# Layer-2 mixers: attention output with features on partitions, scores divided before they are transposed

## The chip, the cores and the metric

The kernel runs on one NeuronCore of a Trainium2 chip. The metric is the device time of one launch in microseconds, the median of several runs. TensorE does the matrix products and the 128 x 128 transposes (into PSUM), VectorE and ScalarE the elementwise work, GpSimd some copies and small products between SBUF buffers, and SyncE issues the DMAs.

## The reference, cut to what matters

Two layers follow each other over 1024 tokens of width 1024. The second layer normalizes its input, projects it, runs three mixers side by side (a windowed attention with a sink, a state-space mixer "ssd" and a gated delta-rule mixer "gdn"), joins their outputs, multiplies them by one output matrix, and adds the normalized result to its input; a feed-forward block follows.

```
s = einsum('bcikgd,bcjkd->bckgij', qc, kb) * (ATT_HEAD_DIM ** -0.5)
s = s - slopes * dist                       # alibi; invalid keys -inf
p = softmax(concatenate([s, sink], -1))[..., :band]
att = einsum('bckgij,bcjkd->bcikgd', p, vb) # 4 heads of 64, 2 kv heads
...
mix = concatenate([att, ssd, gdn], axis=-1) @ w_out      # 256 + 512 + 256 columns
x = x + rmsnorm(mix, post_mix_norm)
```

The change touches the making of `att` and how `att`, `ssd` and `gdn` become the stationary side of the product with `w_out`.

## The kernel before, in words

The whole program is one launch of several stages. The stage in question is `layer2_mixers` (L2185 and on). It works on tiles of 128 tokens, eight of them, in ten steps: `tiles(tile)` calls `tile(n, i, t)` on each engine with n, i = n-1 and t = n-2. The **front** of tile n (attention, the ssd mixer, the preparation of gdn), the **chain** of tile i (the gdn triangular solve by doubling, block size 2, 4, 8, 16, 32, 64, and its state) and the **output product** of tile t (48 float32r matmuls of 128 x 512, as high and low parts) are interleaved. Every engine runs a written order; semaphores with names (`Steps`: `tensF.wait(v, "att", n)` waits until TensorE has done `att` of tile n) tie them. Step 0 has only a front, step 1 a front and a chain, step 8 only a chain and an output; after it stands `end()`.

The chain has two products per level: `level_t(b)` makes T_b, ScalarE copies it, `level_x(b)` makes X_b, VectorE subtracts it (`V`) and turns it (`W`). In the text T64 and X64 are the products of level 64, VT64 is VectorE's copy of X64 (L2778), W the product of `KBG` and `VT` that follows (`wt`), VN the next (`vn`).

TensorE's gaps are filled with output matmuls: `fill(at)` issues those that the table `FILL` gives for that place (`FILL_FIRST` in step 2, `FILL_END` in step 8; in step 1 up to two warming matmuls each). Half 0 of a tile's product begins in one step at "x16" and ends at "end"; its second half starts inside "end", at matmul 24, once ScalarE has copied half 0 out of PSUM (`pc0`, L2454), and this copy waits until VectorE has added the previous tile's residual (`x2`, L2738).

Attention of tile n, in order: four products of queries and keys into PSUM banks 1 and 2 (`scores`), VectorE scales them and adds the bias (`swab`, L2844), maximum (L2847) and differences; ScalarE exponentials with row sums (`e0` to `e3`, L2600) and the sink's (`es`, L2618); TensorE transposes the undivided scores (L3255, `ptr`, right after the level-32 products), ScalarE copies them to `PTR` (`pt`, L2633), TensorE multiplies `PTR` (stationary, 128 columns) by the values (moving, 64 columns), two heads ahead of the ssd product with the state (`yo`, the off-diagonal product) and two heads behind W. VectorE computes the denominator and its reciprocal (L2914, L2916) and writes `att = product * 1/den` with tokens on partitions into `M` (L2927).

`M` holds the 1024 mixer outputs of one tile: 256 of attention, 512 of ssd, 256 of gdn. In the next step TensorE transposes the first six chunks of 128 (`mtrm`) and the last two (`mtrg`, L3179), ScalarE copies them as float32r (`mtm` L2575, `mtg` L2570) and VectorE makes the low part (`mlo` L2835, `mglo` L2722). On VectorE, L (the exponential of the decays `DEC`, made by ScalarE at L2624, `decayed()`) is needed by `nc0` to `nc3` (L2882); in step 0 ScalarE calls `decayed()` behind `pt`, in later steps ahead of it.

## Time and profile before

| | us |
|---|---|
| runs | 2250.68, 2253.72, 2257.84 |
| median of 3 | 2253.72 |
| profiled execution, its time | 2252.55 |
| its span in the profile | 2250.8 |
| TensorE busy over the span | 2207.3 (98%) |
| VectorE busy | 1580.2 (70%) |
| ScalarE busy | 916.0 (41%) |
| GpSimd busy | 260.7 (12%) |
| granted TensorE clock, mean | 0.993 |

Times in the trace are microseconds from the start of the span. Matmul rows overlap, since each shows a matmul until its result is out; the cost of one in a run of them is the distance between starts. An fp32 matmul leaves two rows (records), a transpose and a float32r matmul one. The mixer stage starts at 1286.7 (first transpose of step 0) and the steps' first chain products (T2) stand at 1308.21, 1345.28, 1381.55, 1416.73, 1451.91, 1487.09, 1522.27 and 1557.45; the steady steps 3 to 7 last 35.18 us each.

### The profile page before, as it was taken

To read this page: it belongs to the slowest core of one execution; us is meant where nothing else is said; L and a number is where in the kernel's file an instruction comes from. 1 tells how busy PE (TensorE), PEld (TensorE's weight loads), DVE (VectorE), ACT (ScalarE), POOL (GpSimd) and SP (SyncE) were. 2 spreads that over 40 slices of the span, in tenths; PEclk is the share of its full clock that TensorE was granted. 3 is DMA by queue.
4 is the path that set the end of the run, shared out by engine and by line. 5 is a ranking of instruction groups with operands and counts; after the bars stand their busy time and mean duration, and the time that the engine had idled before them with its cause. 6 is when DMAs were issued, how large, how long until landed. Compare 5 with 4: busy or idle time off the path is not lost. (4 is left out here: it accounts for less than half of the span.)

```text
span 2250.8 us, 34288 instructions
## 1 busy us (share of the span) xinstructions
PE 2207.3 (98%) x13052; PEld 1816.6 (81%) x13052; DVE 1580.2 (70%) x2212; ACT 916.0 (41%) x1672; POOL 260.7 (12%) x266
## 2 busy tenths in 40 slices
PE   8999999999999999999999989999999999999997
PEld 7888888888888888887887767887888888888886
DVE  5657668876665545657687798888798777765557
ACT  5443444343333331233344455555533333324444
POOL 0222232100000000001232232322020000000000
PEclk9999999999999999999999999999999999999999
DMA  4111111134333264433232442323235444448655
GB/s 153 47 38 57 38 50 45 66 132 158 122 113 112 93 248 182 159 113 116 92 113 84 152 169 72 123 77 114 97 129 192 163 158 163 158 157 301 215 181 184
DMA packets 106952, 289.06 MB, mean 128 GB/s; under 512 B 9692, under 2 KB 35388, under 8 KB 102332
## 3 DMA queue, kind: packets, MB, share of 16 engines
q1 hardware_dynamic: 106812, 287.14, 36.4%
q8 instruction: 94, 1.54, 0.3%
q14 instruction: 46, 0.38, 0.0%
HBM read 205.01 MB, written 82.10 MB: 128 GB/s over the span
## 5 line engine op out<-in xcount | busy, mean ns | idle before, releaser
L124 PE MATMUL psG<-h_hi,w_hi 128*128 128x512 f32 (+1 forms) x624 | 164.4, 395 | 4.3 <-DVE features_T L1879 3.9
L124 PE MATMUL psG<-h_hi,w_lo 128*128 128x512 f32 (+1 forms) x624 | 162.2, 392 | 0.0
L124 PE MATMUL psG<-h_lo,w_hi 128*128 128x512 f32 (+1 forms) x624 | 162.2, 393 | 0.0
L455 POOL TENSOR_TENSOR sb_w<-sb_left 128x128 f32<-128x128 f32 (+3 forms) x96 | 96.9, 1014 | 320.8 <-DVE sb_left L582 320.8
L124 PEld LDWEIGHTS psG<-h_hi,w_hi 128*128 128x128 f32 x624 | 110.1, 188 | 25.8 <-DVE features_T L1879 4.7
L124 PEld LDWEIGHTS psG<-h_hi,w_lo 128*128 128x128 f32 x624 | 112.0, 189 | 20.4 <-DVE w_lo L155 0.2
L124 PEld LDWEIGHTS psG<-h_lo,w_hi 128*128 128x128 f32 x624 | 111.6, 189 | 20.2 <-issue 0.5
L582 DVE TENSOR_TENSOR_SCAN sb_left<-sb_left 128x128 f32<-128x128 f32 (+3 forms) x96 | 102.6, 1076 | 2.1 <-ACT sb_left L468 1.4
L155 DVE TENSOR_TENSOR w_lo<-w_raw,w_hi 128x1024 fp32r<-128x1024 f32 x48 | 58.6, 1223 | 55.0 <-ACT w_hi L150 55.0
L150 ACT CAST w_hi<-w_raw 128x1024 fp32r<-128x1024 f32 x48 | 50.3, 1050 | 114.9 <-PE psG L124 62.1
L2028 POOL TENSOR_TENSOR features_T<-m_bias_both 128x512 f32<-128x512 f32 x10 | 16.3, 1635 | 677.3 <-DMA m_bias_both<-in_proj_pairs 630.7
L590 DVE TENSOR_TENSOR sb_w_lo<-psT,sb_w_hi 128x512 fp32r<-128x512 f32 (+1 forms) x80 | 50.0, 625 | 62.1 <-ACT sb_w_hi L476 61.7
L468 ACT ACTIVATE sb_left<-psA 128x128 f32<-128x128 f32 (+3 forms) x96 | 47.2, 491 | 101.0 <-PE psA L124 52.7
L476 ACT CAST sb_w_hi<-psT 128x512 fp32r<-128x512 f32 (+1 forms) x80 | 43.5, 544 | 87.1 <-PE psT L721 87.0
L1051 ACT ACTIVATE features_T<-features_T 128x512 f32<-128x512 f32 x54 | 34.2, 633 | 88.3 <-DVE features_T L1132 87.8
L1916 DVE SCALAR_TENSOR_TENSOR features_T<-features_T,p_par 128x1024 f32<-128x1024 f32 x42 | 55.6, 1323 | 11.5 <-ACT features_T L1780 10.4
L3746 DVE TENSOR_TENSOR h_ffn_lo<-ff_raw_up,h_ffn_hi 128x512 fp32r<-128x512 f32 x49 | 33.7, 690 | 40.8 <-ACT h_ffn_hi L3612 20.6
L3746 DVE TENSOR_TENSOR w_lo<-ff_raw_up,w_hi 128x512 fp32r<-128x512 f32 x39 | 27.0, 692 | 47.0 <-ACT w_hi L3704 47.0
L3746 DVE TENSOR_TENSOR features_T<-ff_y,features_T 128x512 f32<-128x512 f32 x50 | 34.4, 689 | 35.7 <-PE ff_y L124 35.7
L124 PE MATMUL m_ps<-m_w_hi,m_a_hi 128*128 128x512 f32 x128 | 54.1, 433 | 0.4 <-ACT m_raw L2454 0.4
L3612 ACT CAST ff_a_hi<-features_T 128x512 fp32r<-128x512 f32 x40 | 24.6, 625 | 69.6 <-PE psH L124 29.5
L1132 DVE TENSOR_TENSOR features_T<-mg_y,features_T 128x512 f32<-128x512 f32 x45 | 31.0, 689 | 30.4 <-PE mg_y L124 29.9
(657 smaller groups left out, 5931.9 us busy)
## 6 DMA issues: line engine op xcount, KB each, us to landing
w_raw<-in_units SPq DMA_DIRECT2D x76, 512.0 KB, 4.2
w_raw<-hidden_blocks SPq DMA_DIRECT2D x77, 256.0 KB, 2.8
merge_gates<-features_T SPq DMA_DIRECT2D x12, 1024.0 KB, 7.4
merge_gates<-merge_gates SPq DMA_DIRECT2D x12, 1024.0 KB, 4.8
features<-features_T SPq DMA_DIRECT2D x24, 512.0 KB, 6.2
w_spare<-in_units SPq DMA_DIRECT2D x22, 512.0 KB, 4.4
down_sums<-w_spare SPq DMA_DIRECT2D x22, 512.0 KB, 3.3
hidden_blocks<-features_T SPq DMA_DIRECT2D x11, 1024.0 KB, 3.9
```

The source lines that it names most:

```text
L124: return pe.matmul(out, lhs, rhs, start=first, stop=last, skip_group_check=True)
L150: act.copy(self.hi[c % 2][:] if dest is None else dest, self.raw[c % 2][:]).then_inc(self.hi_done, 1)
L155: dve.tensor_tensor(self.lo[c % 2][:] if dest is None else dest, self.raw[c % 2][:], hi.bitcast(F32), ALU.subtract).then_inc(self.lo_done, 1)
L455: pool.tensor_tensor(w, left_chunk(S, 1), left_chunk(S), ALU.subtract).then_inc(w_ready, 1)
L468: act.activation(left_chunk(S), A[:, 0:row_chunk(S)[1]], ACT.Sigmoid, scale=-1.0).then_inc(keep_done, 1)
L476: act.copy(w_hi[n % 2][:, 0:m], wT[n % 2][:, 0:m]).then_inc(w_hi_done, 1)
L582: dve.tensor_tensor_scan(back, back, back, start, ALU.mult, ALU.min).then_inc(scan_done, 1)
L590: dve.tensor_tensor(w_lo[n % 2][:, 0:m], wT[n % 2][:, 0:m], w_hi[n % 2][:, 0:m].bitcast(F32), ALU.subtract).then_inc(w_lo_done, 1)
L1051: act.activation(dst, src, func).then_inc(gated, 1)
L1132: TT = lambda o, a, b, op: dve.tensor_tensor(o, a, b, op)
L1916: dve.scalar_tensor_tensor(acc[r], raw[r][:, t:t + T], par[:, c, t:t + 1], acc[r], ALU.mult, ALU.add).then_inc(step if t else conv_out, 1)
L3746: TT = lambda o, a, b, op: dve.tensor_tensor(o, a, b, op)
```

## The change

1. Attention is made with features on partitions. The values (64 columns) are the stationary side and `PTR` (128 columns) the moving one; head 0 and head 3 go to bank 1 (partitions 0 to 63 and 64 to 127), heads 2 and 1 to bank 2. The rows of `w_out` for attention are put into this order on the host. All four heads are computed in one place, behind the fill "wt" and ahead of W; the off-diagonal product `yo` moves behind W.
2. The scores are divided by the denominator before they are transposed: VectorE's `den` and `rden` move from behind `sd1` and `xdec` to a place ahead of `nc0`, and `pn` (1024 columns) is added there. The score transposes now wait for `pn` and stand behind T64.
3. The two attention chunks need no transpose: ScalarE copies them from banks 1 and 2 to `A0_HI` (`ah`, float32r) and VectorE subtracts (`att`) to `A0_LO`, three buffers each. `M` shrinks to 768 columns, `mtrm`, `mtm` and `mlo` to four chunks.
4. The fill "x64" is emptied into "t64", which now stands ahead of T64 with seven output matmuls.

```diff
+                if front:
+                    tensF.wait(a, "att", n)
+                    if n >= 3:
+                        tensA.wait(a, "a6", n - 3)
+                    scalF.done("ah", a.copy(A0_HI[n % 3][:], PS[:, 1:3, 0:P]))
...
-                    scalG.done("mtm", a.copy(A6_HI[i % 2][:], bank(3, 2)[:, 0:6 * P].rearrange("p (c t) -> p c t", c=6)))
+                    scalG.done("mtm", a.copy(A4_HI[i % 2][:], bank(3).rearrange("p (c t) -> p c t", c=4)))
...
                 if front:
+                    scalF.wait(v, "es", n)
+                    vectF.done("den", tt(den[:], sums[:], es[:], ALU.add))
+                    vectF.wait(v, "den", n)
+                    vectF.done("rden", v.reciprocal(rden[:], den[:]))
+                    vectF.wait(v, "rden", n)
+                    vectF.done("pn", tt(SS[:], SS[:], per(rden[:], AH, 256), ALU.mult))
                     scalL.wait(v, "L", n)
...
-                    scalF.wait(v, "es", n)
-                    vectF.done("den", tt(den[:], sums[:], es[:], ALU.add))
-                    vectF.wait(v, "den", n)
-                    vectF.done("rden", v.reciprocal(rden[:], den[:]))
...
-                    tensF.wait(v, "att", n)
-                    tensG.wait_last(v, "mtrm", n)
-                    vectF.wait(v, "rden", n)
-                    vectF.done("att", tt(heads(M[:, 0:256], AH), heads(PS[:, 1, 0:256], AH), per(rden[:], AH, 64), ALU.mult))
+                    scalF.wait(v, "ah", n)
+                    vectF.done("att", tt(A0_LO[n % 3][:], PS[:, 1:3, 0:P], A0_HI[n % 3][:].bitcast(F32), ALU.subtract))
...
-                def attention(first):
-                    for h in (first, first + 1):
-                        kv = 64 * (h // 2)
-                        mm(PS[:, 1, 64 * h:64 * h + 64], PTR[:, 2 * h], VP[:, kv:kv + 64], True, False)
-                        x = mm(PS[:, 1, 64 * h:64 * h + 64], PTR[:, 2 * h + 1], GA[:, 256 + kv:320 + kv], False, True)
+                def attention():
+                    for pair in ((0, 1), (2, 3)):
+                        for m in range(2):
+                            for h in pair:
+                                kv = 64 * (h // 2)
+                                values = GA[:, 256 + kv:320 + kv] if m else VP[:, kv:kv + 64]
+                                x = mm(PS[half(h), 2 if h in (1, 2) else 1, 0:P], values, PTR[:, 2 * h + m], m == 0, m == 1)
                     return x
...
-                    turn(tensG, "mtrm", 3, [M[:, c * P:(c + 1) * P] for c in range(6)])
+                    turn(tensG, "mtrm", 3, [M[:, c * P:(c + 1) * P] for c in range(4)])
...
-                if front:
-                    for h in range(AH):
-                        if h % 2 == 0:
-                            scalF.wait(pe, f"e{h + 1}", n)
-                        for m in range(2):
-                            x = pe.transpose(PS[:, 1 + h // 2, (2 * (h % 2) + m) * P:(2 * (h % 2) + m + 1) * P], SS[:, h, m * P:(m + 1) * P], C["ident"][:])
-                    tensF.done("ptr", x)
                 if chain and not front:
                     turn_h(1)
                 fill("t64")
                 level_t(64)
+                if front:
+                    vectF.wait(pe, "pn", n)
+                    for h in range(AH):
+                        for m in range(2):
+                            x = pe.transpose(PS[:, 1 + h // 2, (2 * (h % 2) + m) * P:(2 * (h % 2) + m + 1) * P], SS[:, h, m * P:(m + 1) * P], C["ident"][:])
+                    tensF.done("ptr", x)
                 fill("x64")
                 level_x(64)
                 if n == 0:
                     unread(2)
+                if chain and not front:
+                    turn_h(2)
+                fill("wt")
                 if front:
                     scalF.wait(pe, "pt", n)
                     scalF.wait(pe, "ga", n)
                     poolF.wait_last(pe, "vprev", n)
-                    attention(0)
-                    if n == 0:
-                        tensF.done("att", attention(2))
-                        unread(3)
+                    tensF.done("att", attention())
+                if n == 0:
+                    unread(3)
+                if chain:
+
+                    vectG.wait(pe, "VT64", i)
+                    poolG.wait(pe, "kbg", i)
+                    for h in range(GH):
+                        x = mm(PS[half(h), 5, (h // 2) * P:(h // 2) * P + P], KBG[:, 64 * h:64 * h + 64], VT[:, h])
+                    tensG.done("wt", x)
+                if front:
                     vectF.wait(pe, "qkd", n)
                     vectF.wait_last(pe, "st2", n)
                     for g in range(2):
                         x = mm(PS[:, 4, 256 * g:256 * g + 256], BC[:, 2 + g], ST[:, 256 * g:256 * g + 256])
                     tensY.done("yo", x)
...
-FILL = {"x2": (32, 34), "t4": (34, 38), "x4": (38, 42), "t16": (42, 48), "x16": (0, 3), "t32": (3, 7), "x32": (7, 11), "t64": (11, 15),
-        "x64": (15, 18), "wt": (18, 24), "vn": (24, 24), "o": (24, 24), "end": (24, 32)}
+FILL = {"x2": (32, 34), "t4": (34, 38), "x4": (38, 42), "t16": (42, 48), "x16": (0, 3), "t32": (3, 7), "x32": (7, 11), "t64": (11, 18),
+        "x64": (18, 18), "wt": (18, 24), "vn": (24, 24), "o": (24, 24), "end": (24, 32)}
```

## Rows read from the trace of the kernel before

**Rows 1.** Busy us by stretch: PE, PEld, DVE, ACT, POOL, granted clock, DMA, GB/s.

```profile
1308.21:1345.28 37.07, 32.44 (x492) 25.39 (x491) 33.43 (x66) 18.28 (x48) 8.86 (x12) 0.91 0.44 154
...
1451.91:1487.09 35.18, 35.18 (x521) 28.34 (x520) 29.82 (x65) 19.36 (x58) 11.18 (x14) 1.00 0.31 99
```

**Rows 2.** Timeline of TensorE, step 5: start us, length us, instructions.

```profile
1457.90 0.45 PE L3014 MATMUL m_ps<-m_t_blocks,m_vt_blocks 32*32 32x32 f32 x32
...
1470.32 1.09 PE L3255 MATMUL m_ps<-c_ident,m_scores 128*128 128x128 f32 x8
1471.17 0.48 PE L124 MATMUL m_ps<-m_w_lo,m_a_hi 128*128 128x512 f32 x1
...
1472.28 0.67 PE L3014 MATMUL m_ps<-m_v_upper,m_ntr 64*64 64x64 f32 x8
1472.88 0.50 PE L124 MATMUL m_ps<-m_w_hi,m_a_hi 128*128 128x512 f32 x1
...
1473.77 0.68 PE L3014 MATMUL m_ps<-m_vt,m_t 64*64 64x64 f32 x8
...
1475.32 1.08 PE L3014 MATMUL m_ps<-m_ssd_state,m_bc 128*128 128x256 f32 x4
1476.05 0.58 PE L124 MATMUL m_ps<-m_w_hi,m_a_hi 128*128 128x512 f32 x1
...
1477.71 0.66 PE L3014 MATMUL m_ps<-m_vt,m_kbg 128*64 128x128 f32 x8
1478.30 0.43 PE L3014 MATMUL m_ps<-m_v_prev,m_ptr 128*128 128x64 f32 x2
...
1479.24 0.44 PE L3014 MATMUL m_ps<-m_gdn_state,m_wt 128*128 128x128 f32 x2
...
1484.96 0.58 PE L124 MATMUL m_ps<-m_w_hi,m_a_hi 128*128 128x512 f32 x1
```

**Rows 3.** Timeline of VectorE in step 5; idle before in square brackets.

```profile
1469.83 0.96 DVE L2870 COPY m_vt<-m_vt_blocks 32x128 f32<-32x128 f32 x4
1471.46 1.24 DVE L2882 TENSOR_TENSOR m_ntr_blocks<-m_ps,m_dec 32x128 f32<-32x128 f32 x4 [0.68 <-ACT m_dec L2624]
...
1476.24 0.41 DVE L2778 TENSOR_SCALAR m_vt<-m_ps 64x256 f32<-64x256 f32 x1
...
1479.09 0.16 DVE L2914 TENSOR_TENSOR m_softmax<-m_softmax 128x4 f32<-128x4 f32 x1
...
1479.38 0.66 DVE L2920 TENSOR_TENSOR m_y<-m_ps,m_par 128x512 f32<-128x512 f32 x1
...
1480.75 0.42 DVE L2927 TENSOR_TENSOR m_mix<-m_ps,m_softmax 128x256 f32<-128x256 f32 x1
...
1481.91 1.42 DVE L2738 TENSOR_TENSOR m_x<-m_x,m_raw 128x1024 f32<-128x1024 f32 x1
```

**Rows 4.** Timeline of ScalarE in step 5.

```profile
1452.99 0.59 ACT L2524 COPY m_qk<-m_ps 128x512 f32<-128x512 f32 x1 [0.28 <-PE m_ps L3010]
...
1457.13 0.28 ACT L2499 COPY m_t_blocks<-m_ps 128x128 f32<-128x128 f32 x1
...
1472.21 0.99 ACT L2633 COPY m_ptr<-m_ps 128x1024 f32<-128x1024 f32 x1
...
1483.41 0.59 ACT L2454 COPY m_raw<-m_ps 128x512 f32<-128x512 f32 x1 [2.26 <-DVE m_x L2738]
```

**Rows 5.** Timeline of step 0, ScalarE and VectorE.

```profile
1299.12 1.02 ACT L2633 COPY m_ptr<-m_ps 128x1024 f32<-128x1024 f32 x1 [0.65 <-PE m_ps L3255]
...
1300.03 1.49 ACT L2624 ACTIVATE m_dec<-m_dec 128x1536 f32<-128x1536 f32 x1
...
1300.36 0.69 DVE L2784 TENSOR_TENSOR m_xde<-m_xdt,m_par 128x512 f32<-128x512 f32 x1
...
1301.55 1.24 DVE L2882 TENSOR_TENSOR m_ntr_blocks<-m_ps,m_dec 32x128 f32<-32x128 f32 x4 [0.50 <-ACT m_dec L2624]
```

**Rows 6.** Timeline of TensorE, step 2: the score transposes.

```profile
1365.25 1.97 PE L3255 MATMUL m_ps<-c_ident,m_scores 128*128 128x128 f32 x8
```

More of the change, by code:

```diff
@@ L2199, in layer2_mixers @@
         XDT, XDE = front.take("xdt", [P, 512]), front.take("xde", [P, 512])
[L2201 to L2202 removed]
+        A4_HI, A4_LO = ([room.take(f"a_{n}{s}", [P, 4, P], F32R) for s in range(2)] for n in ("hi", "lo"))
+        RAW, X, GP = (room.take(n, [P, D]) for n in ("raw", "x", "gpost"))
+        M = room.take("mix", [P, 768])
+        A0_HI, A0_LO = ([room.take(f"a0_{n}{s}", [P, 2, P], F32R) for s in range(3 if n == "hi" else 2)] for n in ("hi", "lo"))
         GZN, SQO = room.take("gzn", [P, 256]), room.take("sqo", [P, 256])
@@ L3264, in tile @@
                     unread(2)
+                if chain and not front:
+                    turn_h(2)
+                fill("wt")
                 if front:
@@ L3268, in tile @@
                     poolF.wait_last(pe, "vprev", n)
-                    attention(0)
-                    if n == 0:
-                        tensF.done("att", attention(2))
-                        unread(3)
-                    vectF.wait(pe, "qkd", n)
-                    vectF.wait_last(pe, "st2", n)
-                    for g in range(2):
-                        x = mm(PS[:, 4, 256 * g:256 * g + 256], BC[:, 2 + g], ST[:, 256 * g:256 * g + 256])
-                    tensY.done("yo", x)
-                if chain and not front:
-                    turn_h(2)
-                fill("wt")
+                    tensF.done("att", attention())
+                if n == 0:
+                    unread(3)
                 if chain:
@@ L3287, in tile @@
                     tensG.done("wt", x)
-                if front and n:
-                    tensF.done("att", attention(2))
+                if front:
+                    vectF.wait(pe, "qkd", n)
+                    vectF.wait_last(pe, "st2", n)
+                    for g in range(2):
+                        x = mm(PS[:, 4, 256 * g:256 * g + 256], BC[:, 2 + g], ST[:, 256 * g:256 * g + 256])
+                    tensY.done("yo", x)
                 fill("vn")
```

38 lines of the change are left out of this document (20 added, 18 removed).

## The prediction

> **What bounds the kernel now.** I read first the busy time of each engine stretch by stretch, because the change touches one stage only: the layer-2 mixers, where nine steps (0 to 8) run from 1286.7 to 1604 us. A step n handles front tile n, the chain of tile n-1 and the output product of tile n-2. In a steady step TensorE is busy 35.18 of 35.18 us and VectorE 29.82 [rows 1]; steps 3 to 7 all last 35.18. Step 1 is another case: 32.44 of 37.07 us, granted clock 0.91. Next I read TensorE's order of work in one steady step [rows 2]: no row there has an idle time in front of it, so what TensorE no longer does shortens the step, as long as nobody it waits for comes late. Then VectorE's order in the same step [rows 3]: its only pause between X32 and the end of the residual sum is 0.68 us, for ScalarE's exponential of the decays. So VectorE hangs behind TensorE in this half of the step, and what is put into it beyond 0.68 us arrives late at everything after. Last, step 0 [rows 5], where nothing else fills the engines and the longest latency counts.
>
> **TensorE's part (steady step).** (a) Attention product. Before, it is 4 + 4 matmuls of 128 x 64 output, two records each; the second four took 0.94 us (1478.30 to 1479.24), the first four, which end at 1475.32, as long: together 1.88 [rows 2]. After, eight matmuls with 64 stationary columns and 128 moving ones, alternating between the two column halves. The same shape is in the trace: the W product (vt, kbg), eight records in 0.59 us [rows 2]. Twice that, 1.18, is an upper bound, since it pays for the change of shape twice and W, which now stands directly behind attention, has the same shape. For the lower bound: a transpose moves 128 columns too, and eight took 0.85 (1470.32 to 1471.17 [rows 2]), 0.107 each; attention has sixteen such passes, two at a time in the two column halves: 8 x 0.107 = 0.86. I take 0.9, as W pays for the ends anyway: 1.0 saved. Without concurrency of the halves it would be 16 x 0.107 = 1.7 and save 0.2.
> The Trainium skill (TensorEngine Tiling (Array Packing), Performance Considerations) says of a moving side of at most 64 columns: swap the operands and use column tiles, for up to twice the rate. The W rows agree. The same page (Key Properties) says that a change of tiling mode drains the engine, which would speak against it, but here attention and W share the mode.
> (b) The fills (output matmuls of another tile) before and after the 64-level product are merged. Four matmuls took 1.11 (1471.17 to 1472.28), three 0.89 (1472.88 to 1473.77), so one more is about 0.23 and seven together 1.80: 0.20 saved [rows 2].
> (c) The mixer output has four instead of six chunks to transpose: 2 x 0.107 = 0.21 saved.
> TensorE alone: 1.0 + 0.20 + 0.21 = 1.4 us per step.
>
> **VectorE's part.** Added: `pn`, 1024 columns of SBUF times a broadcast reciprocal. The trace has this form at 256 columns with 0.42 and at 512 with 0.69 [rows 3, 5], so 1.05 ns a column and 1.23 us; bounds 1.15 and 1.42 (the 1024-column sum L2738, 1.42, is the slowest of that width [rows 3]). Ahead of it stand `den` and `rden`, moved: with their waits 0.4. They start when the four diagonal copies end (1470.79). The decays come at 1471.46 [rows 3], so what is late is 1470.7 + 0.4 + 1.2 - 1471.46, about 0.8 us (0.7 to 1.1). Everything from `nc0` on is 0.8 late; where `den` and `rden` stood (1479.09 to 1479.38) 0.3 comes back, and 0.5 remains. The low part of the attention chunks replaces the old division at the same size (0.42, nothing); the low part of the rest is a third narrower, which falls before a wait and earns nothing in a steady step.
>
> **ScalarE's part.** `ah`, 256 columns from PSUM; by 0.99 for 1024 and 0.59 for 512 [rows 4] about 0.4. It waits for attention with the copy of W behind it. Attention ends ahead of W, so `ah` runs beside W; cost nothing, 0.2 if it is late. `pt` (0.99) is covered by X64 and six output matmuls, 0.60 + 1.6.
>
> **What is late next.** TensorE's new order from 1470.32: seven output matmuls to 1472.12, T64 (0.60) to 1472.72, the eight score transposes to 1473.57 (`pn` ends at 1472.3, so no wait; 0.4 is the cover), X64, of T64's size, to 1474.18, six output matmuls to about 1475.8, attention to 1476.8. W waits for VectorE's VT64, which started at 1476.24 and took 0.41 [rows 3]; 0.8 late it ends at 1477.45. TensorE stands about 0.65 us. From there: W 0.59, the off-diagonal product 0.73, the VN product starts at 1478.85 instead of 1479.24: of 1.2 us saved by (a) and (b) 0.4 is left. Next, the output group at 1484.96 [rows 2] needs ScalarE's copy `pc0`, which waits for the residual sum; that was done 1.0 us before it was needed (1483.41 + 0.59 = 1484.00 [rows 4]), is now 0.5 late and needed 0.4 earlier: just in time. ScalarE carries the 0.5 on, loses half of it in the pause of 0.28 in front of the q,k copy [rows 4], and its T4 copy (1457.13) then comes about 0.15 too late for X4, which ran at 1457.90 and would now run 0.4 earlier. Sum for a steady step: 0.4 - 0.15 + 0.21 = 0.45 us (bounds: 0, all of it eaten by VectorE and ScalarE; 1.4, nothing eaten). Five steps (3 to 7): -2.2 us, bounds 0 and -7.1.
>
> **Step 0.** Before: score transposes, `pt` 1299.12 to 1300.14, then L (the decays' exponential) from 1300.03 to 1301.52, `nc0` at 1301.55 [rows 5]. The rest of the step is VectorE without a pause, so `nc0` sets its end. In step 0 ScalarE's program has L behind `pt`. After: `pt` waits for the transposes, these for `pn`, and `pn` for VectorE, which is at `xdec` until 1301.05. So: 1301.0 + 0.4 + 1.23 = 1302.6, transposes 0.85 and their tail 0.2 to 1303.7, `pt` to 1304.7, L 1.49 to 1306.2, `nc0` at 1306.2: 4.7 late, less the 0.6 of `den` and `rden` that leave the later part: +4.1. Meanwhile TensorE has nothing to do for 5 us. In the trace the low clock level (1.2 instead of 2.4 GHz) is seen after thin stretches, as in step 2, where the eight transposes took 1.97 instead of 1.09 from first start to last end [rows 2, 6]; if that hits here, 0.8 more. I take +4.6, bounds 3.5 and 6.
> The Trainium skill (TensorE: Matmul & The Clock Gate, Why this matters for your kernels) warns of such gaps between bursts; no row here shows what this one will do.
>
> **Steps 1, 2 and 8.** Step 1 has few output matmuls; its tail runs through TensorE and gains from (a), but VectorE has no 0.68 pause to hide `pn` in (a low-weight split stands there) and is about 1.3 late: -0.5, bounds +1.6 (nothing hidden) and -2.1 (by its clock of 0.91 TensorE spent 0.09 x 37.07 / 0.5 = 6.7 us at the low level [rows 1]; without half of that 1.7 are won). Step 2, likewise without a pause: W waits for VT64 longer than (a) saves: +0.1, bounds +1 and -1.2. Step 8 has no front: only (c), and a narrower split in a latency-bound stretch: -0.3, bounds 0 and -0.7.
>
> **Sum.** 4.6 - 0.5 + 0.1 - 2.2 - 0.3 = +1.7 us. The profiled execution has a span of 2250.8 and a time of 2252.55, so 2254.3; it lies 1.2 below the median of the runs, 2253.72, so the median to expect is 2255.4.
>
> **Rivals.** 1. TensorE's saving comes through whole (chance 0.2). For it: no idle time on TensorE in a steady step. Against: VectorE is 0.8 late at VT64, and that wait is the next one. Then 4.1 - 0.5 - 7.1 - 0.7 = -4.2, with step 2's gain -5.4: 2248.3 to 2249.5. It crosses -0.3% (-6.8 us) only if step 0 also costs 3 or less.
> 2. The other side: the softmax path lies bare at the start (0.13). `pn` is 1.42 and 1.1 late, so steady steps gain under 0.1, and the 5 us without TensorE work bring the low clock to the transposes and to a stretch of step 1: 4.1 + 0.8 + 1.6 + 1.0 - 0.3 = +7.2: 2260.9. It decides from a cost of 6 in steps 0 and 1 together with no gain later.
> 3. The change doesn't do what it says: the column halves don't run beside each other (0.07). Attention takes 1.7; TensorE gets to W at 1477.6 instead of 1476.8, where VectorE would have held it anyway until 1477.45. Steady steps gain 0.3; total +2.3: 2256.
> 4. The forecast: 0.6, own range 2251 to 2259.
> Range of all: from rival 1's lower end 2248 to rival 2's 2261. About 0.3% is what a measurement of this kernel can tell from no change: faster by more than that 0.12 (part of rival 1, if step 0 is cheap too), within 0.78, slower by more than that 0.10.
>
> **What would show it.** A steady step of 34.7 us; TensorE idle in front of the W product, released by VT64 (0.5 to 0.7 us), and a little in front of X4; attention plus W in 1.5 us; `pn` 1.2 us; `nc0` in step 0 some 4.7 us later relative to the first exponentials. Wrong if the steady step is 34.0 or below (VT64 isn't the next wait), if it is 35.2 or more, or if step 0 is less than 3 us longer, which would mean that L isn't behind `pt` in effect.

## The result, and the profile after

The changed kernel takes 2265.78 us in the median of six runs (2262.24 to 2268.63), the kernel before 2252.53 in six runs beside them: ratio 1.0052, 95% interval 1.004 to 1.0064. It is slower by 0.5%, where 2255.4 and "no difference" were forecast; 2265.8 lies outside the range of 2248 to 2261. The profiled execution of after takes 2264.38 us with a span of 2262.5, 11.7 more than before's span.

Busy time by stretch of the changed kernel, steps 0, 1, 2 and 5 (columns as in [rows 1]; the first number behind the stretch is its length):

```profile
1287.60:1314.61 27.01, 20.82 (x133) 16.79 (x134) 18.88 (x35) 13.23 (x26) 8.82 (x15) 0.82 0.67 231
1314.61:1352.02 37.41, 32.22 (x488) 25.03 (x487) 34.31 (x66) 18.36 (x48) 9.99 (x12) 0.86 0.44 152
1352.02:1391.42 39.40, 34.04 (x502) 26.92 (x501) 34.89 (x69) 17.81 (x51) 13.12 (x17) 0.91 0.20 62
1461.98:1497.48 35.50, 34.48 (x519) 27.20 (x518) 32.14 (x65) 19.51 (x58) 11.13 (x14) 1.00 0.29 98
```

| us | before | after | difference | forecast |
|---|---|---|---|---|
| up to the stage's start | 1286.73 | 1287.60 | +0.9 | 0 |
| step 0 (to the first T2) | 21.48 | 27.01 | +5.5 | +4.6 |
| step 1 | 37.07 | 37.41 | +0.3 | -0.5 |
| step 2 | 36.27 | 39.40 | +3.1 | +0.1 |
| steps 3 to 7 | 5 x 35.18 | 34.99, 35.57, 35.50, 35.91, 35.52 | +1.6 | -2.2 |
| step 8 and the rest | | | +0.2 | -0.3 |
| sum | | | +11.7 | +1.7 |

The 0.9 ahead of the stage is code that the change doesn't touch; over all kernels of this study the stage started between 1284.5 and 1289.7, so it says nothing. Of the 10.0 us that lie between the two sums, 3.8 stand in steps 3 to 7, 3.0 in step 2, 0.9 in step 0, 0.9 ahead of the stage and 0.8 in step 1; the rest is step 8 and behind.

TensorE in step 5 (start, length, instructions, in brackets the idle time before and who ended it), to be laid beside [rows 2]. The row with PEld is a weight load:

```profile
1468.49 0.45 PE L3022 MATMUL m_ps<-m_t_blocks,m_vt_blocks 32*32 32x32 f32 x32 [0.45 <-ACT m_t_blocks L2502]
...
1483.08 1.09 PE L3271 MATMUL m_ps<-c_ident,m_scores 128*128 128x128 f32 x8
1484.10 0.68 PE L3022 MATMUL m_ps<-m_vt,m_t 64*64 64x64 f32 x8
...
1486.29 0.44 PE L3022 MATMUL m_ps<-m_ptr,m_v_prev 128*64 128x128 f32 x4
...
1487.96 0.66 PE L3022 MATMUL m_ps<-m_vt,m_kbg 128*64 128x128 f32 x8 [0.57 <-DVE m_vt L2786]
1488.54 1.13 PE L3022 MATMUL m_ps<-m_ssd_state,m_bc 128*128 128x256 f32 x4
1489.51 0.38 PE L3022 MATMUL m_ps<-m_gdn_state,m_wt 128*128 128x128 f32 x2
...
1494.45 1.08 PE L3022 MATMUL m_ps<-m_xde,m_vb 128*128 128x256 f32 x4
1495.44 0.50 PE L124 MATMUL m_ps<-m_w_hi,m_a_hi 128*128 128x512 f32 x1
1495.44 0.19 PEld L124 LDWEIGHTS m_ps<-m_w_hi,m_a_hi 128*128 128x128 f32 x1 [0.31 <-ACT m_raw L2457]
```

The state product of the kernel before:

```profile
1484.23 1.08 PE L3014 MATMUL m_ps<-m_xde,m_vb 128*128 128x256 f32 x4
```

Before, TensorE was busy 35.18 of 35.18 us. After, 34.48, and it waits twice with a bracket: 0.45 ahead of X4 and 0.57 ahead of W. A third wait has its bracket only on the weight load, not on the matmul: from the start of the state product (1494.45) to the next output matmul it is 0.99, before 0.73 (the state product at 1484.23, the output matmul at 1484.96 [rows 2]). The load waits for ScalarE's copy L2457, and this copy is `pc0`. I count the difference, 0.26, as the wait. So the work is 34.22, 0.96 less than before, and the waits are 1.28: the step is 0.32 longer.

VectorE in step 5, beside [rows 3]:

```profile
1481.57 1.22 DVE L2889 TENSOR_TENSOR m_scores<-m_scores,m_softmax 128x1024 f32<-128x1024 f32 x1
...
1487.49 0.41 DVE L2786 TENSOR_SCALAR m_vt<-m_ps 64x256 f32<-64x256 f32 x1
...
1491.13 1.07 DVE L2933 TENSOR_TENSOR m_y<-m_y,m_xd 128x512 f32<-128x512 f32 x1
...
1492.46 1.12 DVE L2936 TENSOR_TENSOR m_ssd_state<-m_ssd_state,m_par 128x512 f32<-128x512 f32 x1
1493.50 1.21 DVE L2746 TENSOR_TENSOR m_x<-m_x,m_raw 128x1024 f32<-128x1024 f32 x1
```

The addition L2933 and the product L2936 were in the kernel before

```profile
1480.14 0.69 DVE L2923 TENSOR_TENSOR m_y<-m_y,m_xd 128x512 f32<-128x512 f32 x1
...
1481.08 0.90 DVE L2928 TENSOR_TENSOR m_ssd_state<-m_ssd_state,m_par 128x512 f32<-128x512 f32 x1
```

Behind the step's start, the copy VT64 begins at 25.51 (1487.49 less 1461.98; before 1476.24 - 1451.91 = 24.33 [rows 3]) and the residual sum ends at 32.73 (before 31.42): 1.2 and 1.3 later. An addition and a product of 512 columns between the two take 1.07 and 1.12; before, they took 0.69 and 0.90.

Step 0, beside [rows 5]:

```profile
1302.24 1.22 DVE L2889 TENSOR_TENSOR m_scores<-m_scores,m_softmax 128x1024 f32<-128x1024 f32 x1
...
1303.52 1.97 PE L3271 MATMUL m_ps<-c_ident,m_scores 128*128 128x128 f32 x8 [4.98 <-DVE m_scores L2889]
...
1305.53 1.01 ACT L2640 COPY m_ptr<-m_ps 128x1024 f32<-128x1024 f32 x1 [6.19 <-PE m_ps L3271]
1306.44 1.49 ACT L2627 ACTIVATE m_dec<-m_dec 128x1536 f32<-128x1536 f32 x1
...
1307.96 1.24 DVE L2896 TENSOR_TENSOR m_ntr_blocks<-m_ps,m_dec 32x128 f32<-32x128 f32 x4 [4.49 <-ACT m_dec L2627]
```

It is the chain of the forecast, link by link; only the transposes ran at the low clock (1.97, against 1.09 at the full one), which the forecast had priced at 0.8.

### The profile page after: what moved, and what is told of

Its sections match the earlier page's. It is cut to its first block and busy times, and to the rows that moved or that the text cites. A ratio compares the mean times of both kernels' runs of the same rounds, so it can differ in the third digit from the quotient of the medians.

```text
span 2262.5 us, 34272 instructions
## 1 busy us (share of the span) xinstructions
PE 2206.7 (98%) x13034; PEld 1812.0 (80%) x13034; DVE 1594.3 (70%) x2220; ACT 916.6 (41%) x1680; POOL 260.6 (12%) x266
## 5 line engine op out<-in xcount | busy, mean ns | idle before, releaser
L2028 POOL TENSOR_TENSOR features_T<-m_bias_both 128x512 f32<-128x512 f32 x10 | 15.9, 1588 | 677.9 <-DMA m_bias_both<-in_proj_pairs 630.5
```

## The experiments

Each ran beside the kernel before on the same chip. Times of steps are from one profiled execution each, which lies anywhere within the few us (up to 11) over which the runs of a kernel scatter, so what is compared are stretches, and whole kernels by their ratios. "Theory 1" to "theory 4" are what the expectations, put down before each run, set against each other.

**1. L first in step 0.** ScalarE's exponential of the decays stands ahead of its copy of the scores there too.

```diff
-                if front and n:
+                if front:
                     decayed()
...
-                    if n == 0:
-                        decayed()
```

> The changed kernel, with one move: in step 0 ScalarE makes L (the exponential of the decays) ahead of the copy pt, as it does in the other steps. Theory 1 (the softmax path lies bare: L waits behind pn, transposes and pt): step 0, 27.0 us in the changed kernel, falls by 2 to 4.5 us to 22.5 to 25; steps 2 to 7 don't change. Theory 2 (the low clock is what costs): step 0 keeps over 26 us, since the gap in TensorE's work stays. Theory 3 (VectorE and GpSimd hold each other up): no change over 0.5 us.

Ratio 1.0034 [1.0023, 1.0046]. Step 0 took 25.75 us, 1.3 less. TensorE's wait for the divided scores stayed at 4.98 and the transposes at 1.97; the wait ahead of the off-diagonal product (0.64 for `qkd` in after) is gone. All three theories missed. In this execution L behind `pt` was worth 1.3 us, and then TensorE itself, which starts late and at the low clock, carries the step. But number 9 has the same order in step 0 and took 27.70 us there: in its profile the low clock (granted 0.50) lay on the stage's first 4.4 us and again from the transposes through attention. So 1.3 us is less than what step 0 differs by from one execution to the next; of the whole kernel only the ratio can be compared.

**2. No division.** The product `pn` is left out, so the attention values aren't normalized.

```diff
-                    vectF.done("pn", tt(SS[:], SS[:], per(rden[:], AH, 256), ALU.mult))
...
-                    vectF.wait(pe, "pn", n)
+                    vectF.wait(pe, "rden", n)
```

> The changed kernel without the multiplication pn (attention is left undivided, so that part of the result is wrong in size); den and rden stay, and the score transposes wait for rden. Theory 1 (VectorE is late by pn, and W, pc0 and X4 wait for it): steady steps fall from 35.5 to 33.8 to 34.2 us, no wait in front of W, step 0 falls by 1.2 to 2, the whole to 2253 or below. Theory 3 (VectorE and GpSimd hold each other up, whatever pn does): steady steps stay at 34.8 or more.

Ratio 1.0002 [0.999, 1.0013]. Its windows of steps 1, 2 and 5:

```profile
1314.45:1348.49 34.04, 29.30 (x488) 22.83 (x488) 32.56 (x63) 17.80 (x48) 9.86 (x11) 0.95 0.48 166
1348.49:1388.79 40.30, 36.81 (x502) 29.00 (x501) 34.37 (x70) 18.46 (x51) 13.20 (x17) 0.83 0.19 61
1457.95:1492.84 34.89, 34.40 (x519) 27.20 (x518) 31.14 (x64) 19.47 (x58) 11.15 (x14) 1.00 0.31 100
```

The wait ahead of W is gone, that ahead of X4 stays (0.49), and so does that for `pc0` (1.00 from the state product to the next output matmul). The steady step is 34.89, which is theory 3's number (34.8 or more) and not theory 1's; of the changed kernel's 35.50 only 0.6 is the division's. With no division at all, in this order of work, the change only comes level with before. The profiled run, 2259.29, was the longest of its ten, and steps 1 and 2 of it, 74.34 together, have the low clock in step 2 (granted 0.83). Step 0 was 25.76: of its 4.3 us over before, 3.9 stand ahead of the transposes (14.67 us behind the stage's start instead of 10.78), where TensorE idles 3.72 us for the reciprocal alone.

**3. GpSimd's products cut to one column** (`xd`, `vprev`, `vbt`, `kbg` and the copy of B and C, `keep0`, each from the second tile on, so the rest of their results is left out). One of the five:

```diff
-                    poolF.done("vprev", copy(g, VP[:], GA[:, 256:384], zero))
+                    poolF.done("vprev", copy(g, VP[:], GA[:, 256:384], zero) if n == 0 else copy(g, VP[:, 0:1], GA[:, 256:257], zero))
...
```

> The changed kernel with five GpSimd operations (xd, vprev, vbt, kbg and the copy of B and C) cut to one column from the second tile on: the same instructions and waits, but next to no time on GpSimd (results of ssd, attention and gdn are wrong for it). Theory 3 (contention: single VectorE rows such as the sum behind yo grew from 0.69 to 1.07, the small ysc from 0.36 to 0.87): VectorE's busy time in a steady step falls from 32.15 to under 31.2 us, and the step from 35.5 to 35.0 or below. Theory 1 alone: busy time falls too, but the step stays within 0.2 us of 35.5, since the lateness is set by pn.

Ratio 1.0018 [1.0006, 1.003]. The window of step 5:

```profile
1461.84:1496.66 34.82, 34.25 (x519) 27.28 (x518) 30.53 (x66) 19.56 (x60) 7.60 (x14) 1.00 0.31 100
```

Three rows of VectorE's timeline in it, the small product at the step's start and the addition and the product behind VT64:

```profile
1465.48 0.65 DVE L2809 TENSOR_SCALAR small_cols<-small_cols 128x2 f32<-128x2 f32 x1
...
1490.48 0.69 DVE L2933 TENSOR_TENSOR m_y<-m_y,m_xd 128x512 f32<-128x512 f32 x1
...
1491.42 0.68 DVE L2936 TENSOR_TENSOR m_ssd_state<-m_ssd_state,m_par 128x512 f32<-128x512 f32 x1
```

The addition and the product took 1.07 and 1.12 in the changed kernel. The small product, in the changed kernel with GpSimd's full `keep0` copy beside it and in the kernel before, was

```profile
1466.08 0.87 DVE L2809 TENSOR_SCALAR small_cols<-small_cols 128x2 f32<-128x2 f32 x1 [0.49 <-ACT m_mix L2543]
```

```profile
1455.55 0.36 DVE L2801 TENSOR_SCALAR small_cols<-small_cols 128x2 f32<-128x2 f32 x1
```

VectorE's busy time falls by 1.6, to 30.53, though it does the same work, and the step to 34.82: the waits at X4 and `pc0` are gone (from the state product to the next output matmul 0.73 again), the one at W stays (0.57). The residual sum ends 31.40 behind the step's start, as before the change (31.42). So the division makes W wait, and the collisions with GpSimd make X4 and `pc0` wait. Theory 3 holds for those two. The division isn't needed for the collisions: without it (number 2) the addition and the product took 1.08 and 1.12 as well.

**4. Warm transposes in step 0.** Nine matmuls whose results nothing reads, ahead of them.

```diff
+                if n == 0:
+                    unread(9)
                 if front:
                     vectF.wait(pe, "pn", n)
```

> The changed kernel with nine unread matmuls (some 4.7 us) ahead of the score transposes of step 0, where TensorE stood for 4.98 us. Theory 2 (low clock): the transposes take 1.09 instead of 1.97 us, step 0 falls by 0.9 us or more, step 1 by up to 1. Theory 1: step 0 falls by no more than the transposes' 0.9 us, since L still waits for pt.

Ratio 1.0058 [1.0038, 1.0078]. The transposes ran at the full clock, and step 0 took 27.80 in this execution, nothing won. TensorE's timeline:

```profile
1305.53 1.09 PE L3273 MATMUL m_ps<-c_ident,m_scores 128*128 128x128 f32 x8 [1.09 <-DVE m_scores L2889]
...
1311.71 1.13 PE L3022 MATMUL m_ps<-m_ssd_state,m_bc 128*128 128x256 f32 x4 [1.39 <-DVE m_qkd L2901]
1312.90 2.83 PE L3022 MATMUL m_ps<-m_xdt,m_sd 128*128 128x64 f32 x16
1315.53 2.02 PE L3022 MATMUL m_ps<-m_xde,m_vb 128*128 128x256 f32 x4
```

What TensorE gained, it gave back waiting for `qkd` (1.39, after 0.64), and then the low clock came anyway, 7 us behind the transposes, and stretched 2.00 to 2.83 and 1.08 to 2.02 (2.00 and 1.08 in after).

**5. VectorE's part alone, in the kernel before.** `den` and `rden` in the new place, and a maximum over the scores, 1.22 us, in place of the division; nothing reads it.

```diff
                 if front:
+                    scalF.wait(v, "es", n)
+                    vectF.done("den", tt(den[:], sums[:], es[:], ALU.add))
...
+                    vectF.done("pn", v.tensor_reduce(quads[:, 7, :], SS[:], AX, ALU.max))
                     scalL.wait(v, "L", n)
```

> The kernel before with VectorE's part of the change alone: denominator and reciprocal moved ahead of the chain's products, and behind them a maximum over the 128x1024 scores (1.22 us, as long as the division), whose result nothing reads; TensorE's work and order, and the attention, stay as before. Theory 1 (what the steady steps lose is VectorE's lateness alone): the steady step goes from 35.18 us to about 35.7 to 36.2, since TensorE keeps the 1.4 us of work that the change saves it, and its waits (product of the 64 blocks, W) appear as in the changed kernel; the whole kernel comes out at 2255 to 2259 us. In steps 0 and 2 little is lost (under 1 us each), since the transposes don't wait for it there. Theory 3 (VectorE is late because it shares with GpSimd): VectorE's busy time in a steady step rises by more than the reduce's 1.2 us, to over 31.5 us. If the steady step stays within 0.2 us of 35.18, the lateness of VectorE isn't what the changed kernel pays for, and both theories fall.

Ratio 1.0031 [1.0018, 1.0043]: slower without any of TensorE's changes, and not where I looked for it. The windows of steps 1, 2 and 5:

```profile
1306.34:1345.04 38.70, 33.81 (x492) 26.43 (x492) 34.17 (x67) 18.34 (x48) 9.40 (x12) 0.87 0.41 147
1345.04:1383.72 38.68, 33.94 (x504) 26.50 (x503) 34.71 (x68) 17.22 (x49) 12.57 (x16) 0.96 0.19 63
1454.11:1489.35 35.24, 35.24 (x521) 28.33 (x520) 31.89 (x66) 19.27 (x58) 11.65 (x14) 1.00 0.30 99
```

VectorE's timeline in the last of them:

```profile
1479.39 0.41 DVE L2778 TENSOR_SCALAR m_vt<-m_ps 64x256 f32<-64x256 f32 x1
...
1484.66 1.42 DVE L2738 TENSOR_TENSOR m_x<-m_x,m_raw 128x1024 f32<-128x1024 f32 x1
```

The steady step is 35.24, so theories 1 and 3 as I had put them fall for it, though VectorE's busy time did rise by more than the maximum, to 31.89, as theory 3 had it: VectorE is 0.95 late at VT64 (25.28 behind the step's start, 24.33 before) and 0.55 at the residual sum, and TensorE, with its old amount of work, hardly notices (0.06). It has just that much room: VT64 ends at 25.69 and W starts at 25.87. But steps 1 and 2 lose 1.6 and 2.4 us, 4.0 together, where the changed kernel loses 3.5. Nothing but VectorE's part was changed for it. This execution, 2255.85, is one of the shortest of its ten, which reach to 2265.26; the longer ones have the lower mean granted clock (0.994 here, 0.986 to 0.989 from 2260 on). Where those lose the rest, no profile shows.

This gave theory 4: in a steady step VectorE's row of work up to VT64 and TensorE's are nearly equally long. TensorE's saving is real but becomes a wait for VectorE's VT64.

**6, 7 and 8. The division on GpSimd.** In 6 at the same place (with L first in step 0); in 7 also with `den` and `rden` ahead of the decay mask; in 8 also with the splits of weight chunks 2 and 7 behind VectorE's products for the chain.

```diff
+                    vectF.wait(g, "rden", n)
+                    poolF.done("pn", g.tensor_tensor(SS[:], SS[:], per(rden[:], AH, 256), ALU.mult))
```

> The changed kernel with the division on GpSimd (idle for 11 us there) in place of VectorE, at the same place behind the reciprocal, and in step 0 ScalarE's decay exponential ahead of its copy of the scores. Theory 1: VectorE's busy time in a steady step falls to that of the run without the division (31.1 us) and the steady step to about 34.9; but the transposes get their scores later by the difference of the two engines (GpSimd takes about 2 us for 128x1024 by its 1.04 us for 128x512), 0.9 us later than in the changed kernel, which was just in time: so steady steps between 34.9 and 35.7, step 0 at 26 to 27. Theory 3: the division on GpSimd runs beside VectorE's products and makes those longer; VectorE's busy time stays at 31.6 or more and the step at 35.5 or more.

> As the run before this one, with denominator and reciprocal moved on VectorE ahead of the decay mask, so that GpSimd's division can start 1.8 us earlier (steps 1 to 8) and 2.3 us earlier (step 0). Theory 1 (VectorE's lateness in the steady steps, the wait for the divided scores in step 0): steady steps at 34.9 (35.1 at most), step 0 at 23 to 24.5 (the transposes wait until about 14.5 us behind the stage's start in place of 15.9), the whole kernel at 2254 to 2258 us. Theory 2 (step 0 is long because of the low clock): step 0 falls by over 3 us only if its transposes run at the full clock (1.09 us in place of 1.97); with the low clock it stays over 24.5.

> As the run before this one, with VectorE's split of a low weight chunk in step 1 (chunk 2) and step 2 (chunk 7) moved from ahead of the chain's products to behind them. Theory 1 (step 2 lost 3.1 us because the split, 1.23 us, and the division stand ahead of everything that TensorE waits for there, and the waits bring the low clock): step 2 falls to 36.5 to 38 us and step 1 by 0 to 1 us. Theory 2 (the low clock falls where it will, whatever VectorE's order): step 2 stays at 38.5 us or more.

Ratios 1.004 [1.0025, 1.0055], 1.0053 [1.0035, 1.007] and 1.004 [1.0018, 1.0062]. Steady steps 35.34 (in 6), 36.21 and 36.22 (in 7 and 8); step 0 25.39, 26.04 and 24.60. In 6, which came out within theory 1's bounds for the steady step, W no longer waits, but the transposes do (0.41), and X4 still (0.47). GpSimd's division in 6:

```profile
1480.46 1.89 POOL L2426 TENSOR_TENSOR m_scores<-m_scores,m_softmax 128x1024 f32<-128x1024 f32 x1 [8.69 <-DVE m_softmax L2888]
```

In 7, with VectorE's decay mask and diagonal copies:

```profile
1478.86 1.73 DVE L2877 SCALAR_TENSOR_TENSOR m_dec<-m_dec,m_masks 128x1536 f32<-128x1536 f32 x1
...
1479.02 3.32 POOL L2426 TENSOR_TENSOR m_scores<-m_scores,m_softmax 128x1024 f32<-128x1024 f32 x1 [6.27 <-DVE m_softmax L2875]
...
1480.51 2.66 DVE L2883 COPY m_vt<-m_vt_blocks 32x128 f32<-32x128 f32 x4
```

In the changed kernel the same copies:

```profile
1480.17 0.96 DVE L2878 COPY m_vt<-m_vt_blocks 32x128 f32<-32x128 f32 x4
```

Put early, it ran into two operations of VectorE: it took 1.4 us longer beside the decay mask, and VectorE's copies behind it 1.7 longer, until it was done. So 7 missed its 34.9 by 1.3 us. The Trainium skill (SBUF — State Buffer, Who interferes with whom) says that a VectorE instruction with two SBUF inputs, or a copy in one of its two-port modes, contends with a GpSimd instruction that reads SBUF, and that the one issued second waits until the first is done. The row of the mask agrees: 1480.59, the mask's end, plus 1.89 is 1482.48, and the division ends at 1482.34. In which mode the copies ran isn't shown; they end 0.83 behind the division, where all four alone take 0.96. In 8 step 1 fell to 35.86 (37.70 in 7), but step 2 stayed at 39.28 (39.64 in 7), against theory 1's 36.5 to 38; theory 2 had 38.5 or more.

**9. TensorE's order around W.** First attention pair, off-diagonal product, W, second pair; `ah` behind the copy of W; L first in step 0. Between the lines shown stand the off-diagonal product and W.

```diff
-                    tensF.done("att", attention())
+                    attention((0, 1))
...
+                if front and n:
+                    tensF.done("att", attention((2, 3)))
```

> The changed kernel with TensorE's order around W mended: first attention pair, the off-diagonal product (0.97 us), W, second attention pair, and ScalarE's rounded copy of the attention behind its copy of W; in step 0 ScalarE's decay exponential ahead of its copy of the scores. Theory 4 (the steady step of the changed kernel is TensorE's 34.5 us of work and three waits of 1.28 us together, of which the one in front of W, 0.57, stands there because VT64 comes when VectorE is done and what could cover it was moved behind W): TensorE's wait in front of W falls to 0.3 or less, the wait for VT64 stays where it is, relative to the step's start, and the steady step falls by 0.3 to 0.4 us, to 35.1 to 35.2. Rival (the end of the step is set by VectorE's own row of work up to the residual sum, whatever TensorE does around W): the steady step stays at 35.4 to 35.6, and the wait only moves to the output group behind the state product or to X4.

Ratio 1.0027 [1.0012, 1.0043], steady step 35.22, as theory 4 had it. VT64 ends at 1487.25 and W starts at 1487.30, 26.01 behind the step's start (25.98 in after) but with no bracket: TensorE works up to it. What was won is that 0.5 us of attention now lies behind W. Left are 0.48 at X4 and the wait for `pc0`, where the weight load stands 0.31 as in after.

**10 and 11. The division on ScalarE**, head by head, with the score transposes behind the 64-level product and W ahead of attention, denominator and reciprocal directly behind the decay mask, `ah` behind the copy of W, three output matmuls moved, and the two splits moved as in 8. In 11 the root (two small activations) also stands ahead of the copy `pt` in ScalarE's queue; those are the last added lines.

```diff
+                def divided(first):
+                    vectF.wait(a, "rden", n)
+                    for h in (first, first + 1):
+                        scalF.done(f"p{h}", a.activation(SS[:, h], SS[:, h], ACT.Copy, scale=rden[:, h:h + 1]))
...
+                if front and prod is not None:
+                    root(prod)
                 if front:
                     tensF.wait(a, "ptr", n)
```

> The changed kernel with the division on ScalarE, head by head (four activations with the reciprocal as scale, about 0.41 us apart as the exponentials are), so that neither VectorE nor GpSimd has it; denominator and reciprocal directly behind the decay mask; in step 0 the division ahead of the decay exponential; three of the output matmuls between T64 and the 64-level product, the score transposes behind that, W ahead of attention; the low-weight splits of chunks 2 and 7 behind the chain's products. Theory 4 (VectorE's order is what the waits hang on; GpSimd's division failed because it shares with VectorE): VectorE's busy time in a steady step 31.2 us, as without the division, the wait in front of W gone or under 0.2, the steady step 34.5 to 34.9; step 0 at 23 to 24.5 (first transposes 14.5 to 15 us behind the stage's start), steps 1 and 2 together 73 to 75.5 (76.8 in the changed kernel, 73.3 before), the whole kernel at 2252 to 2256. Rival (the division's place on the way from exponentials to transposes is what costs, on any engine): the transposes wait in every step, for ScalarE now, and the steady step stays at 35.4 or more.

> As the run with the division on ScalarE, but ScalarE's logarithm and exponential of the rest's root stand ahead of the copy of the turned scores in its queue, where they stood behind it. In that run W waited 2.38 us for VT64, and VectorE itself stood 1.58 us in front of the post-norm product, which is ahead of VT64, for that root. Theory 4 (three orders that hold each other up; the copy of the turned scores was the one in the way): W's wait goes below 0.5 us, the steady step falls from 36.5 to 34.4 to 34.9 us, and with steps 0 to 2 at 97 us in sum (94.8 before) the whole kernel stands at 2248 to 2254, level with the kernel before. Rival (the division in the path is what costs, on whichever engine): the steady step stays at 35.5 or more and the kernel 8 us or more over the kernel before.

10: ratio 1.0051 [1.0034, 1.0068], steady step 36.47 and, twice, 38.11 and 38.35 with low clock (granted 0.96). Here theory 4's number missed, and the timelines of VectorE and TensorE in step 5 tell why:

```profile
1482.63 1.28 DVE L2752 SCALAR_TENSOR_TENSOR m_raw<-m_raw,small_cols,m_gpost 128x1024 f32<-128x1024 f32 x1 [1.58 <-ACT small_cols L2467]
...
1484.29 0.66 PE L3031 MATMUL m_ps<-m_vt,m_kbg 128*64 128x128 f32 x8 [2.38 <-DVE m_vt L2797]
```

VectorE, ahead of VT64, waits for a root that in ScalarE's queue stood behind the copy of the turned scores, which I had moved back. With the root ahead of it (11): ratio 1.0001 [0.9993, 1.001], step 0 in 23.69, and these windows of steps 1, 2 and 5:

```profile
1312.89:1349.41 36.52, 32.60 (x491) 25.37 (x490) 32.49 (x63) 20.00 (x52) 9.31 (x12) 0.86 0.44 154
1349.41:1387.79 38.38, 34.85 (x503) 27.59 (x502) 33.63 (x68) 19.52 (x55) 13.13 (x17) 0.87 0.20 63
1457.37:1492.16 34.79, 34.11 (x519) 27.19 (x518) 29.50 (x65) 21.23 (x63) 11.19 (x14) 1.00 0.32 100
```

The steady step is 34.79, 0.39 less than before the change and within theory 4's bounds; VectorE's busy time is 29.50. One wait is left (0.68 at W, where theory 4 had under 0.5).

**12. Number 11 with TensorE's idle times of steps 0 to 2 filled** by matmuls that nothing reads: the lines shown ahead of the products of queries and keys, three more ahead of level 32 in step 2, four ahead of T64 in step 1, two ahead of X64 in both, and ten in step 0.

```diff
+                if n in (1, 2):
+                    vectF.wait(pe, "swab", n)
+                    warm(1 if n == 1 else 3)
...
+                if n == 0:
+                    unread(10)
```

> The run before this one with TensorE's idle times of steps 0 to 2 filled by matmuls whose results nothing reads (0.26 us each at the full clock: ten ahead of the score transposes of step 0, where it idled 3.33 us; seven in step 1, eight in step 2, each ahead of a wait of 0.3 to 1.3 us). Theory 2 (what steps 0 to 2 still lose against the kernel before, 98.6 us in place of 94.8, is the low clock that thin stretches bring: granted 0.86, 0.86 and 0.87 there, 0.94, 0.91 and 0.95 before): the granted clock of steps 1 and 2 rises to 0.95 or more, their sum falls from 74.9 to 71.5 to 73 us, and the kernel stands 2 to 4 us below the kernel before. Theory 1 (the low clock is a passenger; VectorE's row of work bounds these steps, busy 32.5 and 33.6 us in them): the sum of steps 1 and 2 changes by less than 1 us, and the kernel stays level with the kernel before.

The windows of steps 1 and 2:

```profile
1310.20:1344.81 34.61, 31.57 (x505) 24.62 (x504) 32.58 (x64) 20.11 (x52) 9.71 (x12) 1.00 0.46 164
1344.81:1381.58 36.77, 34.57 (x519) 27.32 (x518) 33.67 (x68) 19.52 (x55) 13.14 (x17) 1.00 0.21 66
```

Granted clock 1.00 in steps 1 and 2, and their sum 71.38 instead of 74.90 (73.34 before the change): in this execution theory 2 comes within 0.1 of its bounds (71.5 to 73). The whole kernel doesn't: 2254.14 in the median of 11 runs, ratio 0.9999 [0.9989, 1.0009]. The profiled run, 2251.12, was one of the shorter. No version here beats the kernel before by more than can be measured; 11 and 12 are level with it and by medians, taken in other sets of runs, 10 and 12 us faster than the changed one.

## Why the prediction was wrong

**Step 0** (forecast +4.6 of 3.5 to 6, came +5.5). Right up to `nc0`, and within its bounds. `pn` ends 15.86 us behind the stage's start; the working gives 1302.6 - 1286.73 = 15.9. `nc0` is 5.5 later, not 4.7, and the 0.8 is the low clock on the transposes, which the text priced and half believed. Behind `nc0` one term was wrong: the 0.6 that the text took off for `den` and `rden` never came back. They stood behind `qkd`, and from `qkd` on it isn't VectorE that sets the step's end but TensorE: from the off-diagonal product to the end of the step it took 4.04 us before (1304.17 to 1308.21) and 4.04 after (1310.57 to 1314.61). Run 1 puts the order of L and `pt` at 1.3 us only, in one execution: behind it TensorE's late start is nearly as long.

**The steady step** (forecast -0.45, bounds -1.4 to 0; came +0.32, steps 3 to 7 +1.6). The mechanism, TensorE's saving met by waits for late engines, is what the rows show; three terms of its sum were looked at, and two were mis-sized.
- TensorE's saving: 1.4 in the text, 0.96 measured. Attention went from 1.88 to 1.10 (1486.29 to about 1487.39), not to 0.9; the mixer's transposes gave their 0.21, the merged fills 0.18 (2.00 to 1.82) and the six fills ahead of W 0.08. But two products got another neighbour: the off-diagonal product took 0.97 to the next start instead of 0.73, the score transposes 1.02 instead of 0.85. These 0.41 us I had at nothing. The 0.12 that is left of the 0.96 lies in differences of under 0.1 each.
- Wait ahead of W: 0.65 in the text, 0.57 measured. The place was right; that the size was, is luck: VT64 ended 25.92 behind the step's start and not 25.54, and TensorE was ready for W at 25.41 and not at 24.89, since it had already waited 0.45 at X4. A part of the 0.4 was in the reading: the text has the diagonal copies end at 1470.7, and by its own row it is 1470.79; run 5 has VT64 0.95 late for VectorE's part alone, not 0.8.
- X4 and `pc0`: 0.15 and nothing in the text ("just in time"), 0.45 and 0.26 measured. This is the step of the working that failed. The residual sum comes 1.3 late, not 0.5. Run 5 shows that 0.5 was right for the division alone (0.55). Run 3 shows what is added: VectorE works beside GpSimd's `vbt`, `vprev`, `kbg`, which were beside other operations before, and an addition and a product cost 0.6 more, of which the residual sum gives 0.2 back. At the step's start the small product ahead of X4's chain took 0.87 (0.65 in run 3, so at least 0.22 of it is such a collision; before it took 0.36, and the rest isn't explained). Without these collisions both waits are gone. They don't hang on the division alone: run 2, without it, has them all, and both waits, and run 5, with the division's time but TensorE's old order, has only the one at the small product (0.86) and no wait. That TensorE's new order is what brings the others about is argued from these two runs; no run shows it by itself.

So work is 0.96 less (1.4 forecast), waits are 1.28 more (0.95 follows from the text). The lower bound "0, all of it eaten" was wrong as a bound. I had let waits eat the saving and nothing else; but waits at different places add up, and each is paid by an engine that is late for its own reason.

**Steps 1 and 2** (forecast -0.5 and +0.1, came +0.3 and +3.1). Failed for step 2, outside its bounds (+1). I counted only the wait for VT64 there. Run 5 shows 4.0 us for both steps with nothing but 1.6 us of VectorE work in front of the chain's products. That step 2 is long is no accident of one execution: it took 39.67 in number 4 and 39.72 in number 9, which have the changed kernel's step 2 or nearly so. In step 2 of after the waits pile up along the way from there:

```profile
1373.95 0.67 PE L3022 MATMUL m_ps<-m_v_upper,m_ntr 64*64 64x64 f32 x8 [1.18 <-ACT m_v_upper L2514]
1375.82 1.96 PE L3271 MATMUL m_ps<-c_ident,m_scores 128*128 128x128 f32 x8 [1.20 <-DVE m_scores L2889]
```

The transposes wait for `pn` here, since VectorE's split of a weight chunk stands ahead of it, and TensorE then goes on at the low clock (granted 0.50 from 1375.9 to 1382.7). Between the profiled executions of 11 and 12 the clock and its waits are worth 3.5 us in these two steps. How much of after's 3.5 is clock and how much wait wasn't separated.

**The rivals.** Rival 1 (the saving whole) is out by the waits, and rival 3 (no concurrency of the column halves) because attention took 1.10 us, where one half after the other would have been 1.7. Rival 2, slower at the start with the low clock and steady steps that gain under 0.1, had the right side and 0.13 of the chance; it gave 2260.9 and was still 5 short: its steady steps could only stop gaining, not lose (+1.6), it had 1.0 for step 2 (+3.1), and its 1.6 for step 1 came as 0.3. To a slowdown of over 0.3% the text gave 0.10.

**Left open.** What filling the waits is worth. The mean granted clock was 0.993 to 0.996 in all eleven runs of 12 and 0.987 to 0.991 in all twelve of 11, so the effect on the clock is there each time; but the medians differ by 1.4 us only, where the two profiles differ by 5.7. A part of the scatter is the clock itself: of the kernel before's runs beside the experiments, the 14 with a mean granted clock of 0.994 took 2252.3 in the median and the 19 with 0.991 took 2256.9. The changed kernel's six runs had 0.987 to 0.993. How much of its 0.5% of extra time is the clock, and whether the clock fell because of the waits, no run separates. Why steps 1 and 2 granted 0.91 and 0.95 before, with idle times of about 1 us in both, while after they granted 0.86 and 0.91, is not told by any row. Nor is the one steady step in most kernels that is 0.3 to 0.8 us longer than the others (35.91 in after).

## What to carry to other kernels

Where two engines are nearly equally long in a step, shortening one can come back as a wait of about the same size: look first at how much room the other has (here 0.18 us between VT64 and W once VectorE was late). Price a delay not only at the next wait but at each later wait of the cycle, and add them; VectorE work that is moved in time meets other GpSimd work. Put an added operation on the engine that has room, and then check what that engine's queue holds behind it: with the division in different places and orders the step took 35.3 or 36.2 us on GpSimd, 35.5 on VectorE, 36.5 on ScalarE, and 34.8 on ScalarE with one small root moved ahead of one copy.

## What the runs showed of the hardware

- A 128x1024 product on GpSimd took 1.89 us in number 6, and 3.32 in number 7, where it starts beside a VectorE product with two SBUF inputs; four VectorE copies behind it took 2.66 instead of 0.96.
- The low clock also comes where no idle time is long. In number 11 no wait of TensorE in steps 1 and 2 is over 1.3 us, and 0.86 and 0.87 were granted; with fifteen matmuls in these waits (and ten more in step 0), 1.00. The Trainium skill (TensorE: Matmul & The Clock Gate, Why this matters for your kernels) warns of long idle gaps between bursts of matmuls; steps 1 and 2 of number 11 have none, so to keep clear of such gaps wasn't enough here.
- Filling one gap can move the low clock instead of removing it (number 4, in one execution: from the transposes to the products 7 us later).
- The time of a run goes with its mean granted clock: the kernel before took 2252.3 us in the median of 14 runs at 0.994 and 2256.9 in that of 19 runs at 0.991.
- What a product costs hangs on what stands behind it: the off-diagonal product (four records, 128x256) took 0.73 us to the next start with an output matmul behind it and 0.97 with the smaller VN product; eight transposes took 0.85 with an output matmul behind them (before, and in number 11) and 1.02 with X64.
- A wait for a copy out of PSUM can be missing from the matmul's row and stand on its weight load only (0.31 at 1495.44 of after).
